# Routing of a mixture of experts in one fused block: where the norm weights are applied, how ranks are summed, and what is made first

## The chip, the cores and the metric

The kernel runs on one core of a Trainium2 chip (trn2) as one program. The metric is its time on the device in microseconds (us), lower is better. Every input and output is float32.

## The reference, cut to what matters

T = 512 tokens of width D = 1024 go through two blocks. The first ends with a two-level router and 32 experts, of which each token uses two; the change lies there. The second block (feed-forward, attention, feed-forward) isn't touched.

```python
x = x + (g_a * y_a + g_b * y_b) @ w_out + b_out          # residual, before the experts
h = rms_norm(x, norm_ffn_g)                              # x / rms(x) * norm_ffn_g
g_logits = h @ w_rg + b_rg                               # 4 groups
g_sel, g_w = argmax(g_logits), softmax(g_logits)[g_sel]
e_logits = (h @ w_re + b_re)[group g_sel]                # 8 experts of that group
top_v, top_i = top_k(e_logits, 2)
e_w = softmax(top_v) * g_w
for the two experts e of a token:
    x += e_w * ((silu(h @ w_gate[e]) * (h @ w_up[e])) @ w_down[e])
```

## The kernel before

The whole program has five queues written out by hand, one per engine: TensorE (PE), VectorE (DVE), ScalarE (ACT), GpSimd (POOL) and SyncE (SP), which issues the loads. Every order between engines is a semaphore wait in that code; `dlink` (in the routing called `link`) makes an instruction of DVE wait for the one before it on DVE.

**Residual rows.** The last product of the first part, `x1 = x + mix @ w_out`, is made in two halves of 512 columns. `mul_rows` (L579) takes one chunk of two k-tiles of weights and multiplies four tiles of 128 tokens (t), in order k-tile outer, token tile inner; so all four banks of PSUM are finished only at the chunk's end, and `residual_rows` (L1056) waits for that end and adds the rows four times. ACT then squares each tile with a sum (L1335) and copies transposed tiles (L1339); PE transposes (L1204) and multiplies by the router weights (`logits_part`, L1194), into bank 0. The router weights `wr` were multiplied by the norm weights `norm_ffn_g` long before, so the logits need only the scale of each token (`token_scale`).

**Normed rows.** ACT writes x1 times token_scale to `h_tok` (L1344), POOL multiplies that by `g_rows`, the norm weights broadcast to all partitions (L1534), and SP stores each tile to `h_dram` (L1156). `h_tok` lies in the buffer of the third expert's gate and up weights, so the load of these (`load_gate_up(sp, 2, 2)`) comes behind the stores.

**Routing (`dve_moe`).** From the logits DVE finds the group (`first_max`, six linked instructions L1399 to L1404), the expert logits of that group (L1413, L1415), the two largest of these (`first_max` twice), and the one-hot rows of both choices (L1423, sum L1424). PE turns these into ranks: for each token tile t a product with a strictly upper triangle for the tile itself and one with ones for each tile ahead of it, ten products of 32 columns in all (L1213, L1214), and four more for the number of tokens of each expert (L1217). DVE makes from them the number of passes of each expert (a pass is up to CAP = 64 tokens of one expert), their ends, each token's pass and slot (`pos`), and one-hot tables; PE sums the tables (L1222) to the list of tokens in each slot. Meanwhile DVE makes the schedule (L1472 to L1482: which expert and which weight buffer each pass uses), then from the list `scatter_row`, `gather_row` and `row_weight` (L1487 to L1491). With `moe["tables"]` at 1 everything starts: POOL gathers rows of `h_dram` by an indirect DMA (L1550).

**Passes.** Some 37 passes follow, three weight buffers in turn (WSLOTS = 3). For pass n PE transposes the gathered rows (`turn`, L1232), ACT copies them to `xgT` (`pass_`, L1350), PE multiplies gate and up (L1241), ACT applies silu (L1357), DVE multiplies (L1496), PE transposes (L1282), DVE copies (L1500), PE multiplies down (L1249), DVE weighs the rows (L1506), POOL scatters them (L1561). PE's order is: gate and up of n+1 (with the transpose of pass n halfway), `turn(n+2)`, down of n. SP reloads a weight buffer (`reload`, issues at L1125 and L1129) when PE has finished the last pass of the expert in it.

Of the kernel before, what the change touches and what calls it, by code (L numbers as in the profile page):

```python
# [7 lines left out]
P = 128  # L8
T = 512
TT = T // P  # L10
D = 1024
# [11 lines left out]
TOP = 2  # L23
# [9 lines left out]
MARK = -3.3e38  # L33

# [79 lines left out]
def program(nc, A, out):  # L114
    with ExitStack() as ctx:
# [53 lines left out]
        mix_gain = sb("mix_gain", 8)  # L169
        junk = sb("unused_squares", T)  # L170
# [68 lines left out]
        g_rows = sq_[:, :]  # L239
# [54 lines left out]
        x1_r = sem("residual_rows_ready")  # L294
        xt_a = sem("residual_part_read_by_act")
# [230 lines left out]
        def sp_block1(sp):  # L526
# [25 lines left out]
            sp.dma_start(g_rows, row("norm_ffn_g", D)).then_inc(tables_in, 16)  # L552
# [26 lines left out]
        def mul_rows(eng, c0, k, g, xh, xl):  # L579

            s = (c0 + k) % SPLIT
            eng.wait_ge(w_lo, c0 + k + 1)
            for a in range(CK):
                for t in range(TT):
                    f = slice(t * P, t * P + P)
                    o, kt = bank(g, t), 2 * k + a
                    eng.matmul(o, xh[:, kt, f], whi[:, s, a, :], start=(kt == 0), stop=False)
                    eng.matmul(o, xl[:, kt, f], whi[:, s, a, :], start=False, stop=False)
                    mm = eng.matmul(o, xh[:, kt, f], wlo[:, s, a, :], start=False, stop=(kt == KT - 1))
            mm.then_inc(w_used, 1)  # L590
# [513 lines left out]
        n_pass, p_end, p_base = scratch(EXPERTS), scratch(EXPERTS), scratch(EXPERTS)  # L1104
# [36 lines left out]
        def sp_moe(sp):  # L1141
# [18 lines left out]
            sp.wait_ge(moe["tables"], 1)  # L1160
# [37 lines left out]
        def pe_moe(pe):  # L1198
# [132 lines left out]
        def act_moe(act):  # L1331
# [11 lines left out]
            for t in range(TT):  # L1343
                act.activation(h_tok[:, t, :], x1_tok[:, t, :], ACT.Identity, scale=token_scale[:, t, :]).then_inc(rn_r, 1)  # L1344
# [14 lines left out]
            def two(i):  # L1359
                for b in range(2):  # L1360
                    pass2(2 * i + b + 1, 1 - b)
                    pass_(2 * i + b + 2, b)

            pass_(0, 0)
            pass_(1, 1)
            pass2(0, 0)
            act.wait_ge(moe["tables"], 1)
# [6 lines left out]
        def dve_moe(dve):  # L1374
            dve.wait_ge(tables_in, 32)
            dve.tensor_tensor(both_gains, gain_of("norm_final_g"), gain_of("g_ffn1_2"), ALU.mult).then_inc(gain_r, 1)
            residual_rows(dve, 1)
# [19 lines left out]
            def first_max(vals, n, best, where, one_hot, tmp):  # L1397
# [6 lines left out]
                link(dve.tensor_tensor(one_hot, counts(n), bc(where, n), ALU.is_equal))  # L1404
# [7 lines left out]
            dve.tensor_tensor(ex[:, :, 0:GROUPS], gl, bc(g_max, GROUPS), ALU.subtract).then_inc(moe["exp_in"], 1)  # L1412
# [6 lines left out]
            dve.tensor_tensor(ex[:, :, GROUPS:GROUPS + 1], v2, v1, ALU.subtract).then_inc(moe["exp_in"], 1)  # L1419
            for j, i_ in enumerate((i1, i2)):  # L1420
                link(dve.scalar_tensor_tensor(out=i_, in0=g_sel, scalar=float(PER_GROUP), in1=i_, op0=ALU.mult,
                                              op1=ALU.add))
                link(dve.tensor_tensor(hot[j], counts(EXPERTS), bc(i_, EXPERTS), ALU.is_equal))  # L1423
            dve.tensor_tensor(hots, hot[0], hot[1], ALU.add).then_inc(moe["onehot"], 1)  # L1424

# [8 lines left out]
            link(dve.tensor_scalar(over, iota(T // CAP).unsqueeze(1).to_broadcast([P, EXPERTS, T // CAP]), float(CAP), None,  # L1434
                                   ALU.mult))
            link(dve.tensor_tensor(over, psum[:, 1, P:P + EXPERTS].unsqueeze(2).to_broadcast([P, EXPERTS, T // CAP]),
                                   over, ALU.is_gt))
# [7 lines left out]
            for j in range(TOP):  # L1445
                link(dve.tensor_tensor(hot[j], hot[j], place, ALU.mult))
                link(dve.tensor_reduce(pos_f[:, :, j:j + 1], hot[j], AX.X, ALU.add))

                link(dve.tensor_scalar(choice[:, :, j:j + 1], const[:, K_TOK:K_TOK + TT].unsqueeze(2), float(TOP),
                                       j - BIG, ALU.mult, ALU.add))  # L1450
# [6 lines left out]
            dve.wait_ge(moe["h_tok"], TT)  # L1457
# [16 lines left out]
            link(dve.tensor_reduce(e_of, late, AX.X, ALU.add))  # L1474
# [933 lines left out]
```

## Time and profile before

| | us |
|---|---|
| median of 3 runs | 2213.58 (2212.56 to 2214.8) |
| the profiled execution | 2213.56 |
| its span, first to last instruction | 2211.7 |
| around the span | 1.86 |

Busy over the span: PE 2005.0 us (91%), DVE 989.8 (45%), ACT 582.3 (26%), POOL 235.6 (11%). In the strips of 40 slices (55 us each) the DMA engines are busy nine tenths from the tenth slice on to the eighteenth, at 316 to 420 GB/s: these are the experts' weights. The share of busy time says little here: a stage is bounded by whatever ends last in it, and the rows of the section below are read stage by stage. In a timeline a row is start, duration, engine, line, operation, output<-input, and in brackets the idle time ahead of it and who ended it.

### The profile page before, as it was taken

What the parts mean: (1) busy time and instruction counts of PE and PEld (TensorE: products, weight loads), DVE (VectorE), ACT (ScalarE), POOL (GpSimd) and SP (SyncE); (2) the same over time, 40 slices, a digit from 0 to 9 for tenths busy, and PEclk for the clock granted to TensorE, in tenths of its full rate; (3) what the DMA queues carried; (4) which work ended last, traced back from release to release, by engine and by line L of the source; (5) the groups of instructions that cost most, each with busy time, mean ns of one, the idle gap of its engine ahead of it and who ended that gap; (6) DMA issues with size and microseconds to landing.
All of it is one profiled execution on the core that took longest, in us unless ns stands there. A gap on an engine that the chain in (4) does not pass through costs nothing.

```text
span 2211.7 us, 24802 instructions
## 1 busy us (share of the span) xinstructions
PE 2005.0 (91%) x8839; PEld 1377.8 (62%) x8840; DVE 989.8 (45%) x1445; ACT 582.3 (26%) x874; POOL 235.6 (11%) x261
## 2 busy tenths in 40 slices
PE   7999999949888999884999999899788899999998
PEld 6888887833222333223788878776335577888785
DVE  4998954351110111115544432434996444444323
ACT  4235335321000000003222221321327533222212
POOL 2000000021111122113000000201413300000000
PEclk9999999969999999996899999999999999999998
DMA  6432222747999999954233322233000022332221
GB/s 193 149 96 86 86 96 76 290 188 316 419 419 419 420 417 369 420 247 147 77 95 95 95 95 95 86 86 107 20 0 1 1 77 86 95 95 95 94 95 47
DMA packets 145772, 353.36 MB, mean 160 GB/s; under 512 B 26686, under 2 KB 84339, under 8 KB 120490
## 3 DMA queue, kind: packets, MB, share of 16 engines
q1 hardware_dynamic: 139690, 344.06, 42.4%
q0 software_dynamic: 6000, 8.42, 1.1%
q8 instruction: 42, 0.69, 0.1%
q14 instruction: 24, 0.20, 0.0%
q10 hardware_dynamic: 16, 0.00, 0.0%
HBM read 347.96 MB, written 15.73 MB: 164 GB/s over the span
## 4 chain that ended last, share of the span: by engine, by line
PE 71%; DVE 10%; DMA 9%; ACT 4%; issue 2%; POOL 2%; SPq 1%; POOLq 0%; ACTq 0%; DVEq 0%
PE psum L446 17%; PE psum L447 17%; PE psum L448 17%; DMA arena<-in_w_expert_up_dram 8%; PE psum L1241 8%; PE psum L1249 4%; PE psum L1907 2%; DVE w_lo L441 1%; DVE arena L2188 1%; POOL arena L403 1%; DVE stat_mean L2185 1%; PE psum L1936 1%; ACT w_hi L436 1%; PE psum L1232 1%; PE psum L1923 1%
## 5 line engine op out<-in xcount | busy, mean ns | idle before, releaser
L441 DVE TENSOR_TENSOR w_lo<-w_raw,w_hi 128x1024 fp32r<-128x1024 f32 x232 | 292.3, 1261 | 617.3 <-ACT w_hi L436 617.3
L446 PE MATMUL psum<-h_hi,w_hi 128*128 128x512 f32 x1312 | 520.4, 397 | 49.7 <-DVE w_lo L441 18.5
L447 PE MATMUL psum<-h_lo,w_hi 128*128 128x512 f32 x1312 | 517.5, 394 | 0.0
L448 PE MATMUL psum<-h_hi,w_lo 128*128 128x512 f32 x1312 | 516.9, 394 | 0.0
L436 ACT ACTIVATE w_hi<-w_raw 128x1024 fp32r<-128x1024 f32 x232 | 245.8, 1060 | 917.0 <-PE psum L448 872.4
L446 PEld LDWEIGHTS psum<-h_hi,w_hi 128*128 128x128 f32 x1312 | 250.7, 191 | 108.3 <-issue 43.2
L448 PEld LDWEIGHTS psum<-h_hi,w_lo 128*128 128x128 f32 x1312 | 250.5, 191 | 53.3
L447 PEld LDWEIGHTS psum<-h_lo,w_hi 128*128 128x128 f32 x1312 | 250.7, 191 | 52.0 <-issue 0.2
L1241 PE MATMUL psum<-arena,w_raw 128*64 128x512 f32 x832 | 204.0, 637 | 35.2 <-DMA arena<-in_w_expert_up_dram 34.5
L938 DVE SCALAR_TENSOR_TENSOR arena<-arena,vec 128x512 f32<-128x512 f32 x240 | 162.6, 748 | 1.0 <-ACT arena L768 1.0
L1241 PEld LDWEIGHTS psum<-arena,w_raw 128*64 128x64 f32 x832 | 59.9, 145 | 157.3 <-issue 109.2
L446 PE MATMUL psum<-act_hi,w_hi 128*128 (+1 forms) x352 | 137.2, 390 | 3.5 <-DVE gated L1730 3.5
L447 PE MATMUL psum<-act_lo,w_hi 128*128 (+1 forms) x352 | 137.0, 389 | 0.0
L448 PE MATMUL psum<-act_hi,w_lo 128*128 (+1 forms) x352 | 136.9, 389 | 0.0
L1357 ACT ACTIVATE w_raw<-psum 128x256 f32<-128x256 f32 x37 | 14.2, 383 | 444.8 <-PE psum L1241 444.8
L1249 PE MATMUL psum<-arena,w_raw 128*64 128x512 f32 x400 | 91.3, 598 | 0.0
L1500 DVE COPY w_raw<-psum 128x256 f32<-128x256 f32 x36 | 15.3, 425 | 169.5 <-PE psum L1282 169.5
L1241 PE MATMUL psum<-expert_input,w_raw 128*64 128x512 f32 x352 | 81.8, 608 | 9.7 <-DMA expert_input<-in_w_expert_up_dram 9.7
L1506 DVE TENSOR_SCALAR w_raw<-psum,row_weight 128x512 f32<-128x512 f32 x36 | 27.0, 751 | 127.2 <-PE psum L1249 127.2
L1496 DVE TENSOR_TENSOR w_raw<-w_raw,psum 128x256 f32<-128x256 f32 x37 | 15.6, 421 | 148.2 <-ACT w_raw L1357 148.2
L446 PEld LDWEIGHTS psum<-act_hi,w_hi 128*128 128x128 f32 x352 | 66.1, 188 | 18.1 <-DVE gated L1730 4.4
L1561 POOL DMA_INDIRECT expert_rows<-w_raw,scatter_now x36 | 37.0, 1027 | 377.5 <-DVE w_raw L1506 377.5
(306 smaller groups left out, 2171.3 us busy)
## 6 DMA issues: line engine op xcount, KB each, us to landing
arena<-in_w_expert_gate_dram SPq DMA_DIRECT2D x22, 2048.0 KB, 24.5
arena<-in_w_expert_up_dram SPq DMA_DIRECT2D x22, 2048.0 KB, 29.1
arena<-in_w_expert_down_dram SPq DMA_DIRECT2D x22, 2048.0 KB, 22.5
w_raw<-in_w_in_dram SPq DMA_DIRECT2D x44, 512.0 KB, 3.7
w_raw<-in_w_gate_dram SPq DMA_DIRECT2D x88, 256.0 KB, 2.9
w_raw<-in_w_up_dram SPq DMA_DIRECT2D x88, 256.0 KB, 3.1
w_raw<-in_w_down_dram SPq DMA_DIRECT2D x44, 512.0 KB, 3.5
expert_down_third<-in_w_expert_down_dram SPq DMA_DIRECT2D x10, 2048.0 KB
```

The lines of the kernel that those rows point to most:

```text
L403: eng.tensor_tensor(acc, acc, sq[:, (base + k) % 2, :], ALU.add).then_inc(sq_u, 1)
L436: eng.activation(whi[:, (c0 + k) % SPLIT, :, :], raw[:, slot, :, :], ACT.Copy).then_inc(w_hi, 1)
L441: eng.tensor_tensor(wlo[:, s, :, :], raw[:, slot, :, :], whi[:, s, :, :].bitcast(F32), ALU.subtract).then_inc(w_lo, 1)
L446: eng.matmul(o, w_h, x_h, start=first, stop=False)
L447: eng.matmul(o, w_h, x_l, start=False, stop=False)
L448: return eng.matmul(o, w_l, x_h, start=False, stop=last)
L938: dve.scalar_tensor_tensor(out=conv[:, c, :], in0=a_pad[:, c, j:j + T], scalar=conv_w[:, c, j:j + 1], in1=conv[:, c, :], op0=ALU.mult, op1 ...
L1241: mm = pe.matmul(psum[q * CAP:(q + 1) * CAP, 2 + b, :].rearrange("p (w n) -> p w n", w=2), xgT[b][:, k % 4, (k // 4) * CAP:(k // 4 + 1) * ...
L1249: mm = pe.matmul(psum[q * CAP:(q + 1) * CAP, 6 + b, :], heT[b][:, k % 2, (k // 2) * CAP:(k // 2 + 1) * CAP], wd[w][:, k, q * T:(q + 1) * T ...
L1506: dve.tensor_scalar(y_row[b], psum[:, 6 + b, :], w, None, ALU.mult).then_inc(moe["y"], 1)
L1561: pool.indirect_dma_start(y_dram[:, :], bass.IndirectOffsetOnAxis(ap=s_cur[b][:, 0:1], axis=0), y_row[b], None, bounds_check=2 * TOP * T - ...
L1907: pe.matmul(psum[:, u % 2, 0:S], lhs, rhs, start=True, stop=True).then_inc(at_["score"], 1)
```

## The change

1. In `mul_rows` the last chunk of each half takes the token tiles in the outer loop, and a semaphore `row_done` tells when each of the first three banks is finished; `residual_rows` waits for each bank alone.
2. POOL's product with `g_rows` and the broadcast load of `g_rows` go. `h_dram` holds rows without norm weights; the transposed rows are multiplied by `row_gain` where they are read from PSUM. That read moves from ACT (`pass_`, a copy) to DVE (`rows_in`, a product with a broadcast second operand), placed between `product(n+1)` and the weighing of pass n. `row_gain` comes by two DMAs of small elements.
3. `first_max` has five instructions for six; the constants `over`, `choice` and the new `ids` are made ahead of `residual_rows(dve, 1)`; the two differences for the exponential come behind `hots`.
4. The ranks take five products: one with the triangle over 128 columns, three with ones over 96, 64 and 32 columns, and one with ones over 128 columns, whose four parts DVE adds (`n_tok`).
5. `gather_row` is made first, right behind the product of the tables, and lets POOL and PE's first `turn` go (`tables` at 1); `row_weight` and the schedule follow (`tables` at 2), for which SP, ACT, PE's second `turn` and POOL's loop wait. DVE no longer waits for `h_tok`.

```diff
@@ mul_rows
-            for a in range(CK):
-                for t in range(TT):
...
+            tiles_ = [(a, t) for t in range(TT) for a in range(CK)] if k == 3 else \
+                [(a, t) for a in range(CK) for t in range(TT)]
+            for a, t in tiles_:
...
+                if kt == KT - 1 and t < TT - 1:
+                    mm.then_inc(row_done, 1)
@@ residual_rows
-            dve.wait_ge(w_used, C_WO + 4 * half + 4)
             for t in range(TT):
+                if t < TT - 1:
+                    dve.wait_ge(row_done, (TT - 1) * half + t + 1)
+                else:
+                    dve.wait_ge(w_used, C_WO + 4 * half + 4)
@@ sp_block1
-            sp.dma_start(g_rows, row("norm_ffn_g", D)).then_inc(tables_in, 16)
+                for h in range(2):
+                    sp.dma_start(row_gain[:, :].rearrange("p (c h) -> p h c", h=2)[:, h, :],
+                                 A["norm_ffn_g"].rearrange("o (h p c) -> (o h) p c", h=2, c=4)[h]).then_inc(tables_in, 16)
@@ pe_moe
-            for t in range(TT):
-                for q in range(t):
-                    pe.matmul(psum[:, 1, t * 32:t * 32 + 32], ones, hots[:, q, :], start=(q == 0), stop=False)
-                pe.matmul(psum[:, 1, t * 32:t * 32 + 32], const[:, K_UP:K_UP + P], hots[:, t, :], start=(t == 0),
-                          stop=True)
-            for t in range(TT):
-                mm = pe.matmul(psum[:, 1, P:P + 32], ones, hots[:, t, :], start=(t == 0), stop=(t == TT - 1))
+            every = hots.rearrange("p t e -> p (t e)")
+            pe.matmul(psum[:, 1, 0:P], const[:, K_UP:K_UP + P], every, start=True, stop=False)
+            for t in range(1, TT):
+                n = (TT - t) * EXPERTS
+                pe.matmul(psum[:, 1, P - n:P], ones, every[:, 0:n], start=False, stop=False)
+            mm = pe.matmul(psum[:, 1, P:2 * P], ones, every, start=False, stop=True)
...
-            pe.wait_ge(moe["tables"], 1)
             turn(0, 0)
+            pe.wait_ge(moe["tables"], 2)
             turn(1, 1)
@@ act_moe
-            def pass_(n, b):
-                act.wait_ge(moe["x_t"], n + 1)
-                act.activation(xgT[b], psum[:, b, :].rearrange("p (c m) -> p c m", m=P), ACT.Copy).then_inc(
-                    moe["x"], 1)
@@ dve_moe, first_max
-                link(dve.tensor_scalar(tmp, tmp, -99.0, 99.0, ALU.mult, ALU.add))
-                link(dve.tensor_tensor(tmp, tmp, counts(n), ALU.add))
+                link(dve.scalar_tensor_tensor(out=tmp, in0=tmp, scalar=-AWAY, in1=counts(n), op0=ALU.mult, op1=ALU.add))
@@ dve_moe, behind the ranks
+            link(dve.tensor_reduce(n_tok, psum[:, 1, P:2 * P].rearrange("p (t e) -> p e t", e=EXPERTS), AX.X, ALU.add))
@@ dve_moe, behind the table
+            link(dve.tensor_scalar(scatter_row[:, :], slots[:, 0, :], BIG, None, ALU.add))
+            link(dve.tensor_scalar(e_int[:, 0:NPS], scatter_row[:, :], 1, None, ALU.arith_shift_right))
+            dve.tensor_scalar(gather_row[:, :], e_int[:, 0:NPS], 2.0, half, ALU.mult, ALU.add).then_inc(moe["tables"], 1)
+            link(dve.tensor_scalar(scatter_row[:, :], scatter_row[:, :], 2.0, half, ALU.mult, ALU.add))
+            link(dve.tensor_copy(row_weight[:, :], slots[:, 1, :]))
@@ dve_moe, passes
+            def rows_in(n, b):
+                dve.wait_ge(moe["x_t"], n + 1)
+                dve.tensor_tensor(xgT[b].rearrange("p c (h s) -> p c h s", h=2),
+                                  psum[:, b, :].rearrange("p (c h s) -> p c h s", c=4, h=2), gain_bc, ALU.mult).then_inc(
+                    moe["x"], 1)
...
                 product(n + 1, 1 - b)
+                rows_in(n + 2, b)
                 dve.wait_ge(moe["pass"], n + 2)
@@ pool_moe
-                pool.tensor_tensor(h_tok[:, t, :], h_tok[:, t, :], g_rows, ALU.mult).then_inc(moe["h_tok"], 1)
```

## Rows read from the trace of the kernel before

**Rows 1.** Chain of work that ended last, window 425 to 520: start, us, what
```profile
498.95 12.51 PE psum L1241 x48
```

**Rows 2.** SP's timeline: issues of weight loads
```profile
467.15 0.38 SPq L1125 DMA_DIRECT2D expert_input<-in_w_expert_gate_dram  x1
508.22 0.40 SPq L1125 DMA_DIRECT2D arena<-in_w_expert_gate_dram  x1
```

**Rows 3.** SP's waits, window 380 to 1020: total us, times, longest
```profile
SPq L1129 <- PE psum L1249: 315.7, 29, 14.9
```

**Rows 4.** Busy time by stretch: length, busy by engine, PE clock share, DMA share, GB/s
```profile
455.00:458.00 3.00, 0.41 (x4) 0.26 (x3) 2.45 (x4) 3.00 (x4) 2.81 (x2) 0.54 0.01 3
499.00:503.00 4.00, 4.00 (x10) 1.19 (x12) 0.00 (x0) 1.19 (x1) 1.22 (x2) 0.50 0.15 39
560.00:600.00 40.00, 33.03 (x144) 10.99 (x140) 4.42 (x9) 2.94 (x6) 4.97 (x9) 0.96 1.02 418
```

**Rows 5.** Timelines of DVE, ACT and PE: residual rows to logits
```profile
447.19 2.48 DVE L1062 TENSOR_TENSOR xT<-psum,xT 128x512 f32<-128x512 f32 x4 [12.03 <-PE psum L589]
450.45 0.69 DVE L1381 COPY stat_std<-psum 128x512 f32<-128x512 f32 x1 [0.79 <-PE psum L1204]
450.98 0.58 ACT L1339 ACTIVATE stat_mean<-psum 128x512 f32<-128x512 f32 x1
451.61 1.08 PE L1194 MATMUL psum<-w_router,stat_mean 128*128 128x36 f32 x8 [0.98 <-ACT stat_mean L1339]
```

**Rows 6.** DVE's timeline: logits to the first group choice, and the second
```profile
455.79 1.93 DVE L1409 TENSOR_TENSOR w_raw<-w_raw,w_router 128x144 f32<-128x144 f32 x1
462.28 2.27 DVE L1402 TENSOR_TENSOR w_raw<-w_raw,const 128x16 f32<-128x16 f32 x1
464.99 0.18 DVE L1412 TENSOR_TENSOR w_raw<-w_raw 128x16 f32<-128x16 f32 x1
466.26 0.18 DVE L1401 TENSOR_SCALAR w_raw<-w_raw 128x32 f32<-128x32 f32 x1
```

**Rows 7.** POOL's timeline in the same stretch
```profile
455.19 9.32 POOL L1534 TENSOR_TENSOR expert_input<-expert_input,sq 128x1024 f32<-128x1024 f32 x4 [415.59 <-ACT expert_input L1344]
464.46 0.94 POOL L1537 MEMSET arena<- 128x1024 f32 x1
```

**Rows 8.** Timelines of PE and DVE: ranks and table
```profile
470.17 0.63 PE L1214 MATMUL psum<-w_raw,const 128*128 128x32 f32 x2 [14.77 <-DVE w_raw L1424]
476.46 0.29 DVE L1434 TENSOR_SCALAR w_raw<-const 128x256 f32<-128x256 f32 x1 [5.46 <-PE psum L1217]
484.73 3.74 PE L1222 MATMUL psum<-w_raw,sq 128*128 128x104 f32 x16 [8.38 <-DVE w_raw L1466]
```

**Rows 9.** Timelines of DVE and POOL: reduce, constants, schedule, lists of rows
```profile
465.40 0.38 DVE L1415 TENSOR_REDUCE w_raw<-w_raw 128x32 f32<-128x128 f32 x1
479.60 0.17 DVE L1449 TENSOR_SCALAR w_raw<-const 128x4 f32<-128x4 f32 x1
488.17 0.19 DVE L1475 TENSOR_SCALAR w_raw<-w_raw 128x48 f32<-128x48 f32 x1
489.55 0.21 DVE L1487 TENSOR_SCALAR expert_of_pass<-psum 128x52 int32<-128x52 f32 x1
490.87 0.18 POOL L1545 COPY gather_now<-gather_row 128x1 int32<-128x1 int32 x1 [25.46 <-DVE row_weight L1491]
```

**Rows 10.** Timelines of one pass: DVE, ACT, PE; last row from DVE's groups by form
```profile
516.00 0.42 DVE L1496 TENSOR_TENSOR w_raw<-w_raw,psum 128x256 f32<-128x256 f32 x1 [3.64 <-ACT w_raw L1357]
516.20 0.60 ACT L1350 ACTIVATE w_raw<-psum 128x512 f32<-128x512 f32 x1 [0.23 <-PE psum L1232]
519.58 3.60 PE L1241 MATMUL psum<-expert_input,w_raw 128*64 128x512 f32 x16
L1062 DVE TENSOR_TENSOR xT<-psum,xT 128x512 f32<-128x512 f32 x8 | 5.0, 683 | 12.0 <-PE psum L589 12.0
```

**Rows 11.** SP's timeline: a load of small pieces in the first part
```profile
49.42 4.80 SPq L1137 DMA_DIRECT2D w_router<-in_w_router_expert_dram  x1
```

More of the change, by code:

```diff
@@ L169, in program @@
         mix_gain = sb("mix_gain", 8)
+        row_gain = sb("gathered_row_gain", 8)
         junk = sb("unused_squares", T)
@@ L551, in sp_block1 @@
                 load_in(c)
-            sp.dma_start(g_rows, row("norm_ffn_g", D)).then_inc(tables_in, 16)
+            with nc.allow_non_contiguous_dma(reason="gains in the order of the gathered rows"):
+                for h in range(2):
+                    sp.dma_start(row_gain[:, :].rearrange("p (c h) -> p h c", h=2)[:, h, :],
+                                 A["norm_ffn_g"].rearrange("o (h p c) -> (o h) p c", h=2, c=4)[h]).then_inc(tables_in, 16)
             for c in range(14, 18):
@@ L1103, in program @@
         pos_f = scratch(TT, TOP)
-        n_pass, p_end, p_base = scratch(EXPERTS), scratch(EXPERTS), scratch(EXPERTS)
+        n_tok, n_pass, p_end, p_base = (scratch(EXPERTS) for _ in range(4))
+        ids = scratch(EXPERTS)
         NA, NPS = TT * TOP, PASSES + 4
@@ L1374, in dve_moe @@
         def dve_moe(dve):
-            dve.wait_ge(tables_in, 32)
+            dve.wait_ge(tables_in, 48)
             dve.tensor_tensor(both_gains, gain_of("norm_final_g"), gain_of("g_ffn1_2"), ALU.mult).then_inc(gain_r, 1)
+            dve.wait_ge(w_lo, C_WO + 8)
+            for j in range(TOP):
+                dve.tensor_scalar(choice[:, :, j:j + 1], const[:, K_TOK:K_TOK + TT].unsqueeze(2), float(TOP), j - BIG,
+                                  ALU.mult, ALU.add)
+            dve.tensor_scalar(over, iota(T // CAP).unsqueeze(1).to_broadcast([P, EXPERTS, T // CAP]), float(CAP), None,
+                              ALU.mult)
+            dve.tensor_scalar(ids, iota(EXPERTS), -AWAY * (PER_GROUP + 1.0), None, ALU.add)
             residual_rows(dve, 1)
@@ L1422, in dve_moe @@
                                               op1=ALU.add))
[L1423 removed]
+                link(dve.tensor_tensor(hot[j], ids.unsqueeze(1).to_broadcast([P, TT, EXPERTS]), bc(i_, EXPERTS),
+                                       ALU.is_equal))
             dve.tensor_tensor(hots, hot[0], hot[1], ALU.add).then_inc(moe["onehot"], 1)
+            dve.tensor_tensor(ex[:, :, 0:GROUPS], gl, bc(g_max, GROUPS), ALU.subtract).then_inc(moe["exp_in"], 1)
+            dve.tensor_tensor(ex[:, :, GROUPS:GROUPS + 1], v2, v1, ALU.subtract).then_inc(moe["exp_in"], 1)
             dve.wait_ge(moe["exp"], 1)
@@ L1433, in dve_moe @@
             dve.wait_ge(moe["rank"], 1)
[L1434 to L1437, printed above, removed]
+            link(dve.tensor_reduce(n_tok, psum[:, 1, P:2 * P].rearrange("p (t e) -> p e t", e=EXPERTS), AX.X, ALU.add))
+            link(dve.tensor_tensor(over, n_tok.unsqueeze(2).to_broadcast([P, EXPERTS, T // CAP]), over, ALU.is_gt))
             link(dve.tensor_reduce(n_pass, over, AX.X, ALU.add))
@@ L1474, in dve_moe @@
             link(dve.tensor_reduce(e_of, late, AX.X, ALU.add))
+            dve.wait_ge(moe["table"], 1)
+            half = const[:, K_HALF:K_HALF + 1]
+            slots = psum[:, 1, 256:256 + 2 * NPS].rearrange("p (f n) -> p f n", f=2)
+            link(dve.tensor_scalar(scatter_row[:, :], slots[:, 0, :], BIG, None, ALU.add))
[3 more added lines that the diff above has]
+            link(dve.tensor_copy(row_weight[:, :], slots[:, 1, :]))
             link(dve.tensor_scalar(e_of, e_of, float(EXPERTS - 1), None, ALU.min))
+            dve.wait_ge(moe["tables"], 1)
             link(dve.tensor_scalar(e_int[:, 0:PASSES], e_of, 11.0, None, ALU.mult))
@@ L1481, in dve_moe @@
             link(dve.memset(sched[:, S_SLOT + PASSES:S_SLOT + PASSES + 1], (EXPERTS - 1) % WSLOTS))
-            link(dve.tensor_copy(sched[:, S_END:S_END + EXPERTS], p_end))
-            dve.wait_ge(moe["table"], 1)
-            half = const[:, K_HALF:K_HALF + 1]
-            slots = psum[:, 1, 256:256 + 2 * NPS].rearrange("p (f n) -> p f n", f=2)
-            link(dve.tensor_scalar(e_int[:, 0:NPS], slots[:, 0, :], BIG, None, ALU.add))
-            link(dve.tensor_scalar(scatter_row[:, :], e_int[:, 0:NPS], 2.0, half, ALU.mult, ALU.add))
-            link(dve.tensor_scalar(e_int[:, 0:NPS], e_int[:, 0:NPS], 1, None, ALU.arith_shift_right))
-            link(dve.tensor_scalar(gather_row[:, :], e_int[:, 0:NPS], 2.0, half, ALU.mult, ALU.add))
-            dve.tensor_copy(row_weight[:, :], slots[:, 1, :]).then_inc(moe["tables"], 1)
-            dve.wait_ge(moe["tables"], 1)
+            dve.tensor_copy(sched[:, S_END:S_END + EXPERTS], p_end).then_inc(moe["tables"], 1)
+            dve.wait_ge(moe["tables"], 2)
+            gain_bc = row_gain[:, :].rearrange("p (c h) -> p c h", h=2).unsqueeze(3).to_broadcast([P, 4, 2, CAP])
+            def rows_in(n, b):
[3 more added lines that the diff above has]
+                    moe["x"], 1)
             def product(n, b):
@@ L1506, in pass_ @@
                 dve.tensor_scalar(y_row[b], psum[:, 6 + b, :], w, None, ALU.mult).then_inc(moe["y"], 1)
+            rows_in(0, 0)
+            rows_in(1, 1)
             product(0, 0)
@@ L1530, in pool_moe @@
         def pool_moe(pool):
-            pool.wait_ge(tables_in, 32)
-            for t in range(TT):
-                pool.wait_ge(rn_r, 3 * TT + t + 1)
-                pool.tensor_tensor(h_tok[:, t, :], h_tok[:, t, :], g_rows, ALU.mult).then_inc(moe["h_tok"], 1)
             pool.wait_ge(lg_u, KT)
```

33 lines of the change are left out of this document (14 added, 19 removed).

## The prediction

> **What bounds the kernel now.** I read the chain of waits first. In the stretch the change touches it is one thread: the last product's rows, logits, DVE's routing, ranks on PE, routing again, the table, the lists, the gather, and the first gate and up product at 498.95 [rows 1]. Nothing else is under way by then, so this is a serial head.
>
> Next, what the time of that first product sets. The DMA engines stream weights at full share from there on: in 560 to 600 the share is 1.02 and PE is busy 33 of 40 us, so DMA bounds that part [rows 4]. A bound of DMA could swallow a gain ahead of it. But SP's issues say no: the gate and up weights of the third expert go out at 467.15, the next load at 508.22, inside the first pass [rows 2], and SP waits 315.7 us for PE's down products before issues [rows 3]. Every load behind the third expert is let go by a pass, directly or through a chain of passes. So the stream starts when the passes start, and all of it, with what follows, shifts with 498.95. The sum is therefore how much earlier that product starts.
>
> **Step 1, residual rows.** Now PE ends its chunk and then DVE does four additions of 0.68, from 447.19 to 449.67 [rows 5]; ACT's squares follow each, so ACT's first copy starts at 450.98, though DVE's copy of a neighbouring tile could start at 450.45, when PE's transposes are through. PE resumes at 451.61, behind ACT [rows 5]. With three of the four banks done during the chunk, one addition and one square remain behind its end and ACT is free before 450; its copy starts with the transposes, at about 450.4, and PE at 451.0. Worth 0.6 us; bounds 0.4 and 0.8. The transposes are next in line, so nothing more is had.
>
> **Step 2, POOL's product.** The largest term. From 455.79 to 464.55 DVE does four elementwise instructions and one reduce (first and last of the four: [rows 6]). The first takes 1.93 and the last 2.27 us, the latter on 16 elements; the same line's neighbour takes 0.18 on 32 elements a moment later, and one on 16 elements takes 0.18 at 464.99 [rows 6]. POOL's four products run from 455.19 to 464.51, 2.3 us each [rows 7]: DVE's slow instructions end as POOL's do, and the slowness ends with POOL's last. Alone, I price the first (144 elements) at 0.33, from 0.38 for a reduce of 128 [rows 9], and the other four, reduce included, at 0.22 each: 0.18 plus 0.04 for the link (five linked instructions from 489.55 to 490.87 take 0.26 each where the one shown takes 0.21 [rows 9]). That is 1.21 for 8.76, a gain of 7.55 us; bounds 6.6 (if POOL's memset takes its place once, below) and 7.8. ACT's writes of `h_tok` end at about 458 and DVE's slow instructions go on to 464.5, so it isn't ACT.
>
> The Trainium skill ("SBUF — State Buffer", section "Who interferes with whom") states it as a lock: a VectorE instruction with two SBUF inputs, or one in a two-port mode, and a GpSimd instruction that reads SBUF exclude each other for a whole instruction. The trace agrees, down to the 2.3 us. The same section speaks against the change at one place: by it the small one-input instructions that DVE now does while POOL builds its gathers would exclude POOL's writing of descriptors. No row shows that overlap; the rivals price it.
>
> POOL's memset (0.94 us) moves from 464.46 to about 454.8, beside L1408 and L1409. In the run before DVE's instruction at 464.99 (two inputs) lies inside the memset and is short, 0.18 [rows 6, 7]; so I take 0, and 0.9 as the upper bound.
>
> **Step 3, fewer instructions ahead of `hots`.** One of six goes in each of three `first_max`: 3 x 0.22 = 0.66. The two differences (unlinked, half of 0.18 each) go behind `hots`: 0.17. Sum 0.83. Where they went they cost nothing: ACT's exponential and DVE's five small instructions take 0.3 + 0.3 + 5 x 0.2 = 1.6 us beside PE's ranks.
>
> **Step 4, ranks.** Now 14 products, each two instructions in the trace, from 470.17 to 476.46: 6.29 us, 0.225 each all told [rows 8]. Ten remain, up to 128 columns wide. The nearest row is the table's: 16 instructions of 104 columns in 3.74, 0.234 each [rows 8]. So 2.34, and 0.25 for start and end: 2.6. A gain of 3.7; bounds 3.2 (0.28 each, by width) and 4.7, where DVE's 1.6 us would be next. The latter would need PE at full clock; PE's clock share is 0.54 within 3 us of the end of the logits [rows 4], so it is at 1.2 GHz here as before.
>
> **Step 5, between ranks and table.** `over` (0.33) and twice `choice` (0.20 each, from 0.17 [rows 9]) go ahead of the last residual rows, where DVE sat idle for 12 us [rows 5]: cover enough for some 1 us with `ids`. `n_tok` is new: a reduce of 128 elements, 0.38 from SBUF [rows 9], 0.43 to 0.5 with its link and PSUM as source. Net gain 0.73 - 0.45 = 0.3; bounds 0.1 and 0.4. The wait for `h_tok` dropped from DVE was long satisfied.
>
> **Step 6, lists first.** Now the table ends at 484.73 + 3.74 = 488.47 [rows 8], DVE comes to it at 489.55 and POOL starts at 490.87 [rows 9]. After: DVE is free at 488.17 (start of L1475), waits 0.3 for the table, and does three instructions of 0.26: POOL starts 0.85 behind the table, at 489.3 in the old time. Worth 1.55; bounds 1.2 and 1.7. What is late next is the gather itself, which is unchanged. The rest (`scatter_row`, `row_weight`, schedule, eleven instructions of 0.1 to 0.26, 1.8 to 2 us) must be done before PE's second transpose, some 6 us behind POOL's start (490.87 to 498.95 less a transpose and the start): hidden by 4 us.
>
> **Step 7, passes.** ACT's copy of 0.60 becomes DVE's product of 0.68 (L1062, PSUM and SBUF, same size [rows 10]). In the pass shown DVE's product before it ends at 516.42, ACT's copy started at 516.20, and PE needs the result at 519.58 for its next gate and up [rows 10]. DVE's would end at 517.1: 2.5 us of slack, and DVE has nothing until the down product ends at about 519.7. Cost 0 in each of 37 passes, in passes that wait for weights all the more. If the cover were gone it would be 0.1 a pass.
>
> **Step 8, loads.** The two loads of `row_gain` are 1024 pieces of 4 bytes. A load of small pieces held SP 4.8 us [rows 11]; two would hold it up to 10 us around 73. Weights are four chunks ahead at some 5.5 us a chunk, so 0. The stores of `h_tok` need no POOL; the third expert's weights, out at 467.15 before [rows 2], go out at about 460 and are needed 20 us behind the first product: off the path both ways.
>
> **Sum.** 0.6 + 7.55 + 0.83 + 3.7 + 0.3 + 1.55 = 14.5 us. The first gate and up product starts at 484.4. Against the profiled execution, 2213.56: 2199.0. That execution is 0.02 under the median, so it stands for the median as it is.
>
> The clock may add or take some: the first 4 us of gate and up run at half clock before and share 0.50 there [rows 4], and when it rises need not shift with the work. That is 2 us at most either way, and each DMA wait of the stream has such a moment.
>
> **Rivals.**
> (a) *The slow instructions stay.* If their cause were something other than POOL's product, step 2 gives 0 and the gain is 7.0: 2206.6. For it: only coincidence is shown. Against: both ends and the 2.3 us coincide. 4%.
> (b) *POOL's gathers and DVE's table instructions disturb each other*, by the rule above. At worst each of two gathers is held by, or holds, a few instructions of 0.2: 0.5 to 2 us, 2199.5 to 2201. It doesn't leave the range. 10%, within the forecast's range.
> (c) *The gain is lost in the stream.* If the stream's length depended on how far PE had run ahead, some of it comes back; SP's waits speak against, since they are for PE. A half lost gives 2206. 7%.
> (d) *Slower: `rows_in` becomes the bound of a pass.* DVE takes products in order, so x of pass n+2 waits for DVE's product of n+1. The slack is 519.58 - 516.42 = 3.2 us. It decides once `rows_in` takes over 3.2 us, and is slower than before once it costs over 14.5 / 37 = 0.4 a pass more: at 3.6 us, five times the 0.68 of L1062. At 4 us it would be 37 x 0.8 - 14.5 = +15: 2228. Against: no DVE instruction of this size takes over 0.75 when left alone, and it reads SBUF only through the small broadcast gain. 3%.
> (e) *The change doesn't do what it says*: the ranks stay as long because wide products cost by column several times over. Then 3.7 falls out: 2202.7. 3%.
>
> **How the numbers follow.** Forecast, (b) and (e) together 86%: 2196 to 2203, around 2199.0, from the bounds of steps 1 to 6 (11.9 to 16.8 in the worst case together), 2 us of clock and about 1 us of spread of runs. (a) and (c) 11%, 2204 to 2209; (d) 3%. The range that leaves under two in ten out: 2195.5 to 2204.0. 0.2% is 4.4 us, about what a measurement of this kernel can tell from no change: faster is under 2209.2. All of forecast, (a) and most of (c) are: 0.93. Within: 0.04. Slower: 0.03.
>
> **What would show it.** In the trace after: no DVE instruction over 0.4 us between logits and ranks; ten instructions of PE in some 2.6 us; POOL's gather under 1 us behind the table; the first gate and up product near 484.4, and the end of the passes and each later stage earlier by the same 14.5 us. It is wrong if the distance shrinks between the first product and the end of the passes, if PE waits for `rows_in` in a pass, or if DVE's 2 us instructions remain.

## The result: 2232.95 us, slower by 0.9%

| | median, us | runs | ratio to before, 95% interval |
|---|---|---|---|
| before | 2213.07 | 2212.07 to 2214.80 | |
| changed kernel | 2232.95 | 2231.47 to 2233.63 | 1.0086 [1.0074, 1.0098] |
| changed kernel, one buffer less (experiment e5, below) | 2198.65 | 2197.59 to 2199.51 | 0.9921 [0.9907, 0.9934] |

The forecast was 2199.0 with 0.93 for faster. It was wrong by 34 us and in sign. The last row says in advance where this ends: the routing gained about what was forecast, and the place of one 32-byte buffer cost some 34 us, nearly all of it outside the routing.

The chain of waits of the changed kernel, and the timeline of PE, DVE and POOL, show the routing itself (columns: start, us, engine, names or line; what ended the idle time stands in brackets).

```profile
470.11 0.80 PE psum L1224 x2
...
488.69 2.70 DMA arena<-normed_rows,gather_now
...
493.36 13.35 PE psum L1252 x48
```

From the ranks at 470.11 to the first gate and up product at 493.36 are 23.3 us, where the kernel before took 28.8 (470.17 to 498.95 [rows 8, 1]). But the ranks don't start earlier, though the part ahead of them should have given 9 us. SP's issues say where that went. Here is the load that SP issues when PE's last chunk ahead of the routing is through, before and after:

```profile
447.18 0.37 SPq L1129 DMA_DIRECT2D expert_down_third<-in_w_expert_down_dram  x1
```

```profile
456.19 0.37 SPq L1141 DMA_DIRECT2D expert_down_third<-in_w_expert_down_dram  x1
```

The part ahead of the routing ends 9.0 us late. Of the change only the loads of `row_gain`, a few small constants and the new order in two chunks lie ahead of that point. Four moments, each the start of an instruction in the timeline, give the course of the whole:

| | before | changed | changed less before |
|---|---|---|---|
| load of `expert_down_third` goes out | 447.18 | 456.19 | +9.0 |
| first gate and up product of the passes | 498.95 | 493.36 | -5.6 |
| first product of `h_hi` behind the passes | 1022.68 | 1020.25 | -2.4 |
| end of span | 2211.7 | 2230.8 | +19.1 |

The change loses where the dense layers run (9 us in the first 447, 21.5 in the last 1200) and 3 us in the passes between. The heads of the pages name the engine. Changed kernel (PEld is PE's loading of weights):

```profile
span 2230.8 us, 24780 instructions
PE 2034.7 (91%) x8821; PEld 1370.7 (61%) x8822; DVE 1005.4 (45%) x1482; ACT 559.7 (25%) x836; POOL 226.1 (10%) x257
```

before:

```profile
PE 2005.0 (91%) x8839; PEld 1377.8 (62%) x8840; DVE 989.8 (45%) x1445; ACT 582.3 (26%) x874; POOL 235.6 (11%) x261
```

PE is busy for 29.7 us more, with 18 matmuls fewer (the ranks' 28 are 10 now). The dense layers make each product of float32 operands as three products in float32r: both operands are split into a high and a low part (`h_hi`, `h_lo`, `w_hi`, `w_lo`), and the three larger of the four partial products are added. In a row `psum<-h_hi,w_hi` the first name behind the arrow is the moving operand, which streams through PE, and the second the stationary one, loaded into PE as its weights. The groups of instructions (count, busy us, mean ns of one, idle us ahead) show which grew; the kernel before first, then the changed one:

```profile
L446 PE MATMUL psum<-h_hi,w_hi 128*128 128x512 f32 x1312 | 520.4, 397 | 49.7 <-DVE w_lo L441 18.5 <-DVE h_lo L393 16.1 <-ACT stat_std L415 5.3
L446 PE MATMUL psum<-act_hi,w_hi 128*128 x256 | 99.6, 389 | 0.0
```

```profile
L448 PE MATMUL psum<-h_hi,w_hi 128*128 128x512 f32 x1312 | 527.9, 402 | 50.1 <-DVE w_lo L443 18.1 <-DVE h_lo L395 16.9 <-ACT stat_std L417 5.3
L448 PE MATMUL psum<-act_hi,w_hi 128*128 x256 | 101.1, 395 | 0.0
```

The idle time ahead of them is the same; each takes 5 to 6 ns longer. Ends of matmuls are modelled, starts are not, so the starts in the middle of a dense layer decide, before and after:

```profile
1200.89 0.39 PE L447 MATMUL psum<-h_lo,w_hi 128*128 128x512 f32 x1
1201.12 0.39 PE L448 MATMUL psum<-h_hi,w_lo 128*128 128x512 f32 x1
1201.34 0.39 PE L446 MATMUL psum<-h_hi,w_hi 128*128 128x512 f32 x1
1201.57 0.39 PE L447 MATMUL psum<-h_lo,w_hi 128*128 128x512 f32 x1
```

```profile
1200.85 0.40 PE L448 MATMUL psum<-h_hi,w_hi 128*128 128x512 f32 x1
1201.09 0.39 PE L449 MATMUL psum<-h_lo,w_hi 128*128 128x512 f32 x1
1201.32 0.40 PE L450 MATMUL psum<-h_hi,w_lo 128*128 128x512 f32 x1
1201.55 0.39 PE L448 MATMUL psum<-h_hi,w_hi 128*128 128x512 f32 x1
```

0.68 us for three before (0.2267 each), 0.70 after (0.2333). It isn't the clock: PE is granted full clock in both (stretches of the trace; columns: window, its length, PE busy with count, granted clock, DMA share, GB/s). Before, then after:

```profile
1300.00:1400.00 100.00, 100.00 (x443) 1.00 0.29 95
```

```profile
1300.00:1400.00 100.00, 100.00 (x429) 1.00 0.29 91
```

Same clock (1.00, the level of 2.4 GHz), never idle, 14 matmuls fewer in 100 us. Of such products there are 3 x 1312 with `h`, 3 x 352 with `act`, 3 x 128 with `branch` and 3 x 64 with the roles of weights and rows exchanged: 5568. At 0.0067 each that is 37 us, a ceiling since some of it lies beside waits; the busy times of their groups rise by 29.

### The profile page after: what moved, and what is told of

Same layout as the page of the kernel before. It is cut to its first block, busy times and chain, and to the rows that moved or that the text cites. A ratio compares the mean times of both kernels' runs of the same rounds, so it can differ in the third digit from the quotient of the medians.

```text
span 2230.8 us, 24780 instructions
## 1 busy us (share of the span) xinstructions
PE 2034.7 (91%) x8821; PEld 1370.7 (61%) x8822; DVE 1005.4 (45%) x1482; ACT 559.7 (25%) x836; POOL 226.1 (10%) x257
## 4 chain that ended last, share of the span: by engine, by line
PE 73%; DMA 9%; DVE 9%; ACT 4%; issue 2%; POOL 2%; SPq 1%; POOLq 0%; DVEq 0%; ACTq 0%
PE psum L448 18%; PE psum L450 17%; PE psum L449 17%; DMA arena<-in_w_expert_up_dram 9%; PE psum L1252 8%; PE psum L1260 4%; PE psum L1919 2%; DVE arena L2200 1%; DVE w_lo L443 1%; DVE stat_mean L2197 1%; POOL arena L405 1%; PE psum L1948 1%; PE psum L1243 1%; ACT w_hi L438 1%; PE psum L1935 1%
## 5 line engine op out<-in xcount | busy, mean ns | idle before, releaser
L448 PE MATMUL psum<-h_hi,w_hi 128*128 128x512 f32 x1312 | 527.9, 402 | 50.1 <-DVE w_lo L443 18.1
L449 PE MATMUL psum<-h_lo,w_hi 128*128 128x512 f32 x1312 | 524.2, 400 | 0.0
L450 PE MATMUL psum<-h_hi,w_lo 128*128 128x512 f32 x1312 | 523.8, 399 | 0.0
L450 PEld LDWEIGHTS psum<-act_hi,w_lo 128*128 128x128 f32 x352 | 66.0, 187 | 16.2
L449 PEld LDWEIGHTS psum<-act_lo,w_hi 128*128 128x128 f32 x352 | 66.0, 187 | 16.1
```

What stands on the lines that cost most here:

```text
L448: eng.matmul(o, w_h, x_h, start=first, stop=False)
L449: eng.matmul(o, w_h, x_l, start=False, stop=False)
L450: return eng.matmul(o, w_l, x_h, start=False, stop=last)
```

## The experiments

**e1, the changed kernel with the buffer at 64 bytes.**

```diff
-        row_gain = sb("gathered_row_gain", 8)
+        row_gain = sb("gathered_row_gain", 16)[:, 0:8]
```

> The changed kernel with its new buffer of norm weights 16 elements wide instead of 8 (8 used), so that h_hi, h_lo and all behind them lie 64 bytes, not 32, behind their old place. Theory (placement: matmuls of 512 columns start 0.2333 us apart instead of 0.2267 because the new 32-byte buffer moves h_hi and what follows by 32 bytes): spacing back to 0.2267, first gate and up product at 484.4, 2199 us. Rival (the code of the change slows PE, for instance the new order of the last chunk or a semaphore more): spacing 0.2333, 2233 us.

Measured: 2210.79, ratio 0.9986 [0.9973, 0.9998]. 22 us come back for 32 unused bytes, so the rival (the code of the change, 2233) is out. But the expected 2199 is missed by 12 us.

**e2, the kernel before with 32 unused bytes in that place.**

```diff
         mix_gain = sb("mix_gain", 8)
+        sb("unused_8", 8)
```

> The kernel before with nothing but an unused buffer of 8 elements at the same place. Placement: spacing 0.2333 and about 2247 us (2213 plus the 34 us by which the changed kernel missed 2199). Rival (code of the change): 2213 us.

Measured: 2244.27, ratio 1.0133 [1.0113, 1.0154]: slower by 30 with no instruction of the program changed. Its row has the 395 ns of the changed kernel:

```profile
L447 PE MATMUL psum<-act_hi,w_hi 128*128 x256 | 101.1, 395 | 0.0
```

**e3, the same 32 bytes ahead of everything, and e4, 32 bytes ahead of `w_hi` and 32 more behind `mix_gain`.** In e3 both operands move by 32; in e4 `w_hi` by 32 and `h_hi` by 64.

```diff
@@ e3
+        sb("unused_8", 8)
         const = sb("const", K_N)
@@ e4
+        sb("unused_8", 8)
         whi_ = sb("w_hi", SPLIT * CK * CN, F32R)
...
         mix_gain = sb("mix_gain", 8)
+        sb("unused_8b", 8)
```

> The kernel before with an unused buffer of 8 elements ahead of all others, so that w_hi, w_lo and h_hi, h_lo all move by 32 bytes. If what counts is how the weights and the activations lie to each other (modulo 64 bytes): 2213 us. If what counts is where h_hi alone lies: about 2247 us.

> The kernel before with w_hi and w_lo moved by 32 bytes and h_hi, h_lo by 64. If what counts is how the two lie to each other: about 2247 us. If where h_hi alone lies: 2213 us.

Measured: e3 2214.45, ratio 0.9998 [0.9988, 1.0008]; e4 2248.33, ratio 1.0151 [1.0131, 1.0171]. `h_hi` has the same address in e2 and e3, and the times are 30 us apart; `w_hi` has the same address in e3 and e4, and they are 34 apart. So it is neither operand's own place but the distance between them: 32 more is slow in e2 and e4.

**e5, the changed kernel with `h_hi` and all buffers behind it in their old places.** The two one-element buffers `gather_now`, which take 32 bytes each, become two columns of one. That gives back the 32 bytes.

```diff
-        g_cur = [sb(f"gather_now{b}", 1, I32) for b in range(2)]
+        g_both = sb("gather_now", 2, I32)
+        g_cur = [g_both[:, b:b + 1] for b in range(2)]
```

> The changed kernel with its two one-element buffers gather_now0 and gather_now1 as two columns of one buffer, which makes room so that h_hi and all behind it lie exactly where they lay before, in spite of the new buffer. Placement is all of the miss: spacing of 512-column matmuls 0.2267, first gate and up product at 484.4 to 485.2, 2199 to 2200 us. Rival (the product moved to DVE in every pass, or something else in the change, takes back part of it, as the 2210.8 us with a shift of 64 bytes might also mean): 2210 us.

Measured: 2198.65, ratio 0.9921 [0.9907, 0.9934], 34.3 us under the changed kernel. PE's busy time is 2002.2 (2034.7 there), and its row is back:

```profile
L449 PE MATMUL psum<-act_hi,w_hi 128*128 x256 | 99.6, 389 | 0.0
```

This version beats both kernels, and its median lies in the range of the forecast. How much the change gains by it is known to some 3 us: the median is 14.4 us under the 2213.07 of the kernel before, but in e5's own series the kernel before took 2215.44, and the ratio makes it 17.5 (14.6 to 20.6). It is also the run against which the steps of the prediction can be held (below).

**e6, the kernel before without POOL's product.** ACT signals `h_tok` itself and the gathered rows go without their norm weights, so the output isn't the reference's. It prices step 2 of the prediction by itself.

```diff
-            for t in range(TT):
-                pool.wait_ge(rn_r, 3 * TT + t + 1)
-                pool.tensor_tensor(h_tok[:, t, :], h_tok[:, t, :], g_rows, ALU.mult).then_inc(moe["h_tok"], 1)
```

> The kernel before without POOL's product with the norm weights (the rows that are gathered lack the norm weights, so that the output is not the reference's); ACT's writes let the stores go. Theory (POOL's product holds DVE up): no DVE instruction over 0.4 us between logits and ranks, the ranks start 7.5 us earlier, 2213.6 - 7.5 = 2206 us. Rival (the slow DVE instructions have another cause, or a later stage takes it back): 2213 us.

Measured: 2208.35, ratio 0.9966 [0.9953, 0.9978], which is -7.5 us within -10.4 and -4.9; the trace says it more finely. DVE's first instruction takes 0.31 for the 1.93 of before and the one on 16 elements 0.17 for 2.27 [rows 6], and with POOL's memset beside the first it is no longer than forecast (0.33):

```profile
455.32 0.95 POOL L1535 MEMSET arena<- 128x1024 f32 x1 [416.30 <-PE psum L1194]
455.58 0.31 DVE L1410 TENSOR_TENSOR w_raw<-w_raw,w_router 128x144 f32<-128x144 f32 x1
456.54 0.17 DVE L1403 TENSOR_TENSOR w_raw<-w_raw,const 128x16 f32<-128x16 f32 x1
```

POOL's first copy starts at 483.02 for 490.87 [rows 9], the first gate and up product at 491.08 for 498.95 [rows 1]: 7.9 us.

**e7, e8, e9 and e10: other distances, all in the kernel before.** e7 puts 64 unused bytes behind `mix_gain`. The others move `w_hi` and `w_lo` up and leave `h_hi` where it is, by allocating small buffers ahead of `w_raw` and not at their old places behind `mix_gain`: the four one-element buffers (128 bytes), `row_statistics` (256), `unused_squares` (2048).

```diff
@@ e7
         mix_gain = sb("mix_gain", 8)
+        sb("unused_16", 16)
@@ e8, ahead of w_raw
+        g_cur = [sb(f"gather_now{b}", 1, I32) for b in range(2)]
+        s_cur = [sb(f"scatter_now{b}", 1, I32) for b in range(2)]
@@ e9, ahead of w_raw
+        small = sb("row_statistics", 60)
@@ e10, ahead of w_raw
+        junk = sb("unused_squares", T)
```

> The kernel before with an unused buffer of 16 elements, which moves h_hi and what follows by 64 bytes. If the 11.8 us that the changed kernel with a shift of 64 lacked to 2199 us are placement too: 2225 us, spacing between 0.2267 and 0.2333. If 64 bytes are as good as none and the rest of the miss is the change's: 2213 us.

> The kernel before with four one-element buffers moved ahead of w_raw, so that w_hi and w_lo lie 128 bytes further on and h_hi, h_lo where they were. If what counts is the distance of weights and activations modulo 64 bytes alone: 2213 us. If a distance of 128 costs as one of 64 seems to: 2220 to 2230 us.

> The kernel before with row_statistics moved ahead of w_raw, so that w_hi and w_lo lie 256 bytes further on and h_hi, h_lo where they were. If the loss repeats every 64 or 128 bytes it can't be (64 and 128 cost 10 and 27 us); if it repeats every 256: 2213 us; if every 512 or more: 2220 us or more.

> The kernel before with unused_squares moved ahead of w_raw, so that w_hi and w_lo lie 2048 bytes further on. If only the remainder of the distance (by 512 bytes or some other divisor of 2048) counts, as 31744 = 62 x 512 in the kernel before suggests: 2213 us. If the distance itself counts: slower by 10 to 30 us.

All moves of the kernel before together, by what the distance leaves over a multiple of 256 bytes (from `w_*` to `h_*`, `act_*` or `branch_*`):

| over 256 | kernel | us | ratio to before, 95% | mean ns of `act_hi,w_hi` |
|---|---|---|---|---|
| 0 | e3 | 2214.45 | 0.9998 [0.9988, 1.0008] | 389 |
| 0 | e9 | 2214.08 | 1.0002 [0.9992, 1.0011] | 389 |
| 0 | e10 | 2213.53 | 0.9996 [0.9987, 1.0006] | 389 |
| 32 | e2 | 2244.27 | 1.0133 [1.0113, 1.0154] | 395 |
| 32 | e4 | 2248.33 | 1.0151 [1.0131, 1.0171] | 395 |
| 64 | e7 | 2224.90 | 1.0048 [1.0030, 1.0066] | 391 |
| 128 | e8 | 2242.69 | 1.0126 [1.0108, 1.0144] | 395 |

e8 and e9 moved `w` by the same means, 128 and 256 bytes: the one costs 27 us and the other nothing. (The 2242.69 of e8 is above both of its expected times.) e1 belongs to 64: it is 12 us over e5, e7 is 9.5 over the kernel before in its series. In 1300 to 1400 e8 gets 422 matmuls done, in 98.35 us of busy time, and e9 the 443 of before in 100. Here is e8, then e9:

```profile
1300.00:1400.00 100.00, 98.35 (x422) 1.00 0.29 95
```

```profile
1300.00:1400.00 100.00, 100.00 (x443) 1.00 0.31 100
```

The table holds for products with the weights stationary. In the last product of the first part the rows are stationary and the weights move, so that there a distance of 64 is one of -64, which leaves 192 over 256. e7 has it for 3 x 64 products, and they are as slow as those of 32 and 128. So it isn't the size of the distance alone; whether the sign makes this difference or the roles, no run separates. One of the three groups, before and in e7:

```profile
L588 PE MATMUL psum<-w_hi,h_lo 128*128 128x512 f32 x64 | 24.9, 389 | 0.0
```

```profile
L589 PE MATMUL psum<-w_hi,h_lo 128*128 128x512 f32 x64 | 25.3, 395 | 0.0
```

**e11, e5 with `rows_in` as eight products of 64 columns.** This is rival (d) of the prediction, pushed.

```diff
-                dve.tensor_tensor(xgT[b].rearrange("p c (h s) -> p c h s", h=2),
-                                  psum[:, b, :].rearrange("p (c h s) -> p c h s", c=4, h=2), gain_bc, ALU.mult).then_inc(
-                    moe["x"], 1)
+                for c in range(4):
+                    for h in range(2):
+                        o = c * P + h * CAP
+                        ins = dve.tensor_tensor(xgT[b][:, c, h * CAP:(h + 1) * CAP], psum[:, b, o:o + CAP],
+                                                gain_bc[:, c, h, :], ALU.mult)
+                ins.then_inc(moe["x"], 1)
```

> The changed kernel at the old place, with rows_in as eight products of 64 columns instead of one of 512: about 1.8 us instead of 0.7 in each pass. Theory (2.5 us of slack in a pass): 2198.7 to 2200 us. Rival (a pass is bound by rows_in, or DVE's share in the passes costs): 37 x 1.1 = 41 us more, 2240 us.

Measured: 2197.40, ratio 0.9925 [0.9908, 0.9941], the same as e5.

```profile
500.11 0.42 DVE L1513 TENSOR_TENSOR w_raw<-w_raw,psum 128x256 f32<-128x256 f32 x1 [3.65 <-ACT w_raw L1365]
500.44 1.13 DVE L1507 TENSOR_TENSOR w_raw<-psum,gathered_row_gain 128x64 f32<-128x64 f32 x8
503.68 3.60 PE L1253 MATMUL psum<-expert_input,w_raw 128*64 128x512 f32 x16
```

The eight took 1.13 us and not the 1.8 expected, so it presses less than meant. They end at 501.57, 2.1 us ahead of the product that needs them: the slack is real, and 0.45 us more a pass costs nothing.

**e12, the changed kernel with its 32 bytes between `h_lo` and what follows.** The last run asks for both spacings in one kernel: `h_hi` is in its old place again, `act_*`, `branch_*` and the arena stay 32 bytes further up.

```diff
-        row_gain = sb("gathered_row_gain", 8)
...
             hlo_ = c1.enter_context(nc.sbuf_tensor("h_lo", [P, KT * T], F32R))
+            row_gain = c1.enter_context(nc.sbuf_tensor("gathered_row_gain", [P, 8], F32))
```

> The changed kernel with the 32-byte buffer of norm weights placed behind h_hi and h_lo (94112, as before) and ahead of the arena and act_hi, which so stay 32 bytes further up than before. By the theory (the distance between a product's two operands, modulo 256 bytes) this one kernel has both spacings: the 3 x 1312 products of h with w start 0.2267 us apart, and the 3 x 352 of act and the 3 x 128 of branch, whose operands lie behind the buffer, 0.2333 apart. That is 1440 x 0.0067 = 9.6 us over the 2198.7 of the kernel with all buffers in their old places: 2208. By the rival, that the place of the arena or of another buffer behind it sets the spacing of all products, all are slow and the time is 2233; if only h counts, 2199.

Measured: 2207.55, ratio 0.9969 [0.9958, 0.9980]; 8.9 us over e5 by the medians and 10.6 by the two ratios, where 9.6 was expected.

```profile
L448 PE MATMUL psum<-h_hi,w_hi 128*128 128x512 f32 x1312 | 518.7, 395 | 51.3 <-DVE w_lo L443 19.6 <-DVE h_lo L395 16.1 <-ACT stat_std L417 5.3
L448 PE MATMUL psum<-act_hi,w_hi 128*128 x256 | 101.1, 395 | 0.0
```

The products of `h` are as fast as in the kernel before (518.7 for 520.4), those of `act` as slow as in the changed one (101.1 for 99.6). Each product goes by its own two operands; nothing global is slowed.

## Why the prediction was wrong

**The step that failed is none of the eight: it is one that the list lacks.** Step 8 took `row_gain` as "1024 pieces of 4 bytes", two loads whose cover it named, and priced it at 0. The kernel also allocates it with `sb(...)`, ahead of other buffers, and the prediction has no term for that. The opening of the prediction has the same gap: by it the stream "with what follows, shifts with 498.95", and "The sum is therefore how much earlier that product starts." So the dense layers ahead of the routing and behind the passes were put at nothing, and they took 9.0 and 21.5 us more. The missing term is +34.3 us (2232.95 - 2198.65; 36 to 37 by the two ratios to the kernel before). None of the rivals covers it either: the 0.03 for slower was the chance of (d), which did not happen.

**The eight steps**, held against e5, whose span of 2197.6 has the routing undisturbed (the sum: 14.5 forecast, first gate and up product 498.95 - 484.09 = 14.9). The bounds that the steps give add up to 12.3 and 16.2, not to the 11.9 and 16.8 that the prediction states; nothing hangs on it.

```profile
446.93 0.69 DVE L1074 TENSOR_TENSOR xT<-psum,xT 128x512 f32<-128x512 f32 x1 [0.67 <-PE psum L596]
450.74 1.08 PE L1207 MATMUL psum<-w_router,stat_mean 128*128 128x36 f32 x8 [0.36 <-ACT stat_mean L1351]
454.54 0.31 DVE L1419 TENSOR_TENSOR w_raw<-psum,w_raw 128x144 f32<-128x144 f32 x1 [1.54 <-PE psum L1207]
454.56 0.95 POOL L1549 MEMSET arena<- 128x1024 f32 x1 [415.27 <-PE psum L1207]
454.88 0.31 DVE L1420 TENSOR_TENSOR w_raw<-w_raw,w_router 128x144 f32<-128x144 f32 x1
455.63 0.17 DVE L1413 SCALAR_TENSOR_TENSOR w_raw<-w_raw,const 128x16 f32<-128x16 f32 x1
460.84 0.79 PE L1225 MATMUL psum<-w_raw,const 128*128 128x128 f32 x2 [6.34 <-DVE w_raw L1434]
463.45 0.29 DVE L1446 TENSOR_REDUCE w_raw<-psum 128x32 f32<-128x128 f32 x1 [1.23 <-PE psum L1229]
471.29 3.74 PE L1234 MATMUL psum<-w_raw,sq 128*128 128x104 f32 x16 [7.95 <-DVE w_raw L1472]
475.92 0.18 POOL L1557 COPY gather_now<-gather_row 128x1 int32<-128x1 int32 x1 [20.41 <-DVE gather_row L1486]
476.96 0.21 DVE L1493 SCALAR_TENSOR_TENSOR schedule<-schedule,w_raw 128x48 int32<-128x48 int32 x1
477.08 1.24 POOL L1562 DMA_INDIRECT arena<-normed_rows,gather_now  x1 [0.98 <-POOL gather_now L1557]
477.46 0.18 DVE L1497 CAST schedule<-w_raw 128x32 int32<-128x32 f32 x1
484.09 12.86 PE psum L1253 x48
```

| step | forecast | e5 | how read |
|---|---|---|---|
| 1, residual rows | 0.6 | 0.9 | PE resumes at 450.74 for 451.61 [rows 5]; 0.26 of it is that PE's chunk ended earlier |
| 2 and 3, POOL's product, fewer instructions | 8.38 | 8.43 | start of DVE's first routing instruction to ranks: 14.73 (455.44 to 470.17) before, 6.30 (454.54 to 460.84) |
| 4, ranks | 3.7 | 3.7 | 6.29 before, 463.45 - 460.84 = 2.61 (forecast 2.6) |
| 5, between ranks and table | 0.3 | 0.4 | 476.46 to 484.73 before [rows 8], 463.45 to 471.29 |
| 6, lists first | 1.55 | 1.5 | table's start to POOL's copy: 6.14 before [rows 8, 9], 4.63 |
| 7, passes | 0 | 0 | e11, and below |
| 8, loads | 0 | 0 | below |

Step 2: no instruction of DVE between logits and ranks is over 0.38, and the memset (454.56 to 455.51) runs beside the first two, 0.31 each (0.33 was reckoned for the second), so "I take 0" held. The lock that the prediction quoted from the Trainium skill ("SBUF — State Buffer", "Who interferes with whom") is borne out by e6 and e5: take away the POOL instruction that reads, and the slow instructions (1.93 to 2.27 us) are gone; leave the memset, which only writes, and they take 0.17 to 0.31. Step 4: bounds 3.2 and 4.7 were not needed; PE's ten instructions took as long as the row next in kind said.

Step 7, in one of the changed kernel's own passes (36 in the trace; the prediction said 37), where DVE's product of 0.68 ends at 512.27, 2.5 us ahead of its reader, just the slack that was forecast:

```profile
511.25 0.42 DVE L1509 TENSOR_TENSOR w_raw<-w_raw,psum 128x256 f32<-128x256 f32 x1 [3.65 <-ACT w_raw L1364]
511.59 0.68 DVE L1503 TENSOR_TENSOR w_raw<-psum,gathered_row_gain 128x512 f32<-128x512 f32 x1
514.82 3.60 PE L1252 MATMUL psum<-expert_input,w_raw 128*64 128x512 f32 x16
```

Step 8: the two loads held SP for 1.32 us, not for up to 10.

```profile
73.64 1.32 SPq L556 DMA_DIRECT2D gathered_row_gain<-in_norm_ffn_g_dram  x2
```

**The rivals.** (a) fell with e6. (b) did not occur: with POOL making the gather's list and issuing it from 475.92 to 478.32, DVE's instruction at 476.96 takes 0.21 and its one-input cast at 477.46, wholly inside POOL's issue, 0.18; POOL's copy is 0.18 as before, and its issue 1.24. What the prediction took from the Trainium skill (the same section) for this rival found no case here: none of these instructions of DVE was held or held POOL by a measurable time. (c): in e5 the 14.9 us at the first product are 13.0 at the first product of `h_hi` behind the passes (1022.68 - 1009.70) and 14.1 at the end; so up to 2 us went back into the stream and half of it returned. (The DMA engines' nine tenths, named under "Time and profile before", hold from the eleventh to the seventeenth slice; the tenth has seven, the eighteenth five.) (d) did not occur, and e11 gives its slack. (e) fell with step 4.

**The tests named for the trace.** "Each later stage earlier by the same 14.5 us" failed at every moment of the table (-5.6, -2.4, +19.1), so the trace did refute the sum. But all the tests looked at the routing or behind it, and the first 9 us were lost ahead of it. A test of the stretches that the change must *not* move was missing, and would have pointed at PE's products at once.

**What stays open.** That the distance between a product's operands modulo 256 bytes sets the spacing is shown for the remainders 0, 32, 64 and 128, and through the exchanged roles (192 products a run) for 192 in e1 and e7 and 224 in the changed kernel, e2 and e4, all of them 395 ns and more; with the weights stationary these two weren't tried. 96 and 160 weren't tried, nor was any that isn't a multiple of 32. Which of two reads it is that meet, that of the moving operand and that of the next weights, is argued from the fact that only their distance counts; no run separates them. Nor is it known why 64 costs a third of what 32 does, why the exchanged products don't share that, or why at 64 the three products differ (in e1 `act_hi,w_hi` takes 394 and `act_lo,w_hi` 388).

## What to carry to other kernels

A new buffer is an edit to all buffers allocated behind it. Before a change is judged, hold the mean of one in a group that it must not touch, one without idle time, against that of before; if it moved, look at the addresses before looking at the change. Place small buffers behind the large ones, or fill them up so that the large ones move by multiples of 256 bytes; then what is measured is the edit: here a distance put right (e5) turned 0.9% slower into 0.8% faster than before.

## What the runs showed of the hardware

- Back-to-back products of 512 columns in float32r, each with weights of its own, start 0.2267 us apart at full clock if their two operands in SBUF lie a multiple of 256 bytes apart, and 0.2333 us if 32 bytes are left over: 3% of PE's rate. With 128 bytes over the mean of one is the 395 ns of 32, with 64 (moving operand further up) it is 391, and in the products with the roles exchanged, where the same move leaves 192, it is 395 (e7).
- The Trainium skill ("SBUF — State Buffer", "Who interferes with whom") gives PE two read ports, independent of each other, one for the moving operand and one for the weights, and says that PE never waits on anyone. The runs don't agree with that to the last 3%: with no other engine's work changed, e2 and e3 differ by 30 us through the distance of these two operands.
- The products of the expert passes are plain float32 (`arena` with `w_raw`, 832 in the trace). Their distance changed by 32 bytes as well, and the median of one is 592 ns in both kernels; the passes together, from the first gate and up product to the first of `h_hi` behind them, take 526.9 us in the changed kernel and 525.6 in e5. These products don't show the effect, or not over 1.3 us.
- Width costs PE little in the small products of the ranks, at a granted clock of 0.50 (the level of 1.2 GHz) in both kernels: 28 instructions of 32 columns took 6.29 us (0.225 each), ten of 32 to 128 columns 2.61 (0.26 each, e5).
